# Full-width token norms and a block in front of each down projection, in a streaming-encoder layer on one Trainium2 core

## Chip, cores, metric

One NeuronCore of a Trainium2 chip runs the whole layer. The metric is the device time of one execution in microseconds (us); the table below gives the median of three runs. Engines: PE (TensorE, its weight loads shown as PEld), DVE (VectorE), ACT (ScalarE), POOL (GpSimd), SP (here it only issues DMAs).

## The reference

One layer over 2048 tokens, model width 1024, all in float32:

```python
u = rms_norm(h, g_pre_mix)
z_glu, q, k, v, z_gate = split(u @ w_in)
c = a * sigmoid(b)                              # a, b = halves of z_glu
c = silu(layer_norm(causal_depthwise_conv31(c)))
y_conv = c @ w_conv_out
y_attn = banded_attention(rope(q), rope(k), v, sinks) @ w_attn_out
y = gates[0] * y_conv + gates[1] * y_attn       # gates = sigmoid(z_gate)
h = h + rms_norm(y @ w_out, g_post_mix)
gate, val = split(rms_norm(h, g_pre_ffn) @ w_up)     # 2816 columns each
f = (gelu(causal_depthwise_conv3(gate)) * val) @ w_down
h = h + rms_norm(f, g_post_ffn)
h = h + (p @ w_ple) * sigmoid(h @ w_ple_gate)
```

`rms_norm` divides each token's 1024 values by the root of their mean square (plus 1e-6); `layer_norm` also takes the mean off and runs over the 512 convolution channels.

## The kernel before

The sequence is cut into 4 chunks of 512 tokens (`T`). Activations lie with features on the 128 partitions and the 512 tokens along the free axis, so a width of 1024 is 8 tiles of 128x512. Each float32 product is made of three passes: operand and weight are split into a high part (`_hi`, fp32r) and the rest (`_lo`), and `product` (lines 776 to 780) issues hi x hi, hi x lo and lo x hi. A weight **block** is eight 128x128 tiles, so 24 matmuls of 512 columns; a chunk needs `NB` = 122 blocks. `by_tile` (lines 791 to 812) is the form in which four outputs grow together, one input tile after the other.

**Weight stream.** `block_order` (lines 65 to 80) writes out the order of the 488 blocks by hand, `PLACE` is a block's position, and there are `SLOTS` = 3 buffers. SP loads block n once block n-3 is done (`load_block`, lines 376 to 388). In chunk 0 every block is fresh: one load into `w_stage`, POOL makes `w_hi` (line 429, one cast) and `w_lo` (line 432, four subtractions), and SP stores both for the later chunks, which load the two halves directly. PE counts finished blocks in `block_done`, and ACT and DVE wait for that count (`done(c, b)`).

**Token norms.** A sum over features is a sum over partitions. ACT squares each tile (`square`), DVE adds the squares into `ssum` (`add_square`, line 1232). `token_sums` (line 813) makes, with four one-column float32 matmuls (each issued as two), the sums of the 512 tokens as a 128x4 tile in bank `SMALL`; ACT takes the root (line 446), DVE does six small steps on 128x4 (`norm`, line 1202: reciprocal and one Newton step) and spreads the result into four diagonal matrices `diag` (line 1218). Then `spread` (line 821) multiplies `ones` by `diag`, so that bank `BC` holds each token's factor in all partitions. There are four norms of this kind in a chunk (`LN` of the convolution, `POST` after the mixer, `PRE` before and `PF` after the channel mixer), 16 in all. The norm of the input rows (`x_norm`) works on rows and has no matmul.

**Channel mixer.** 22 up tiles (`up(c, t)`), each two blocks, gate and value. For each one ACT starts the 3-tap convolution (line 609), DVE ends it (lines 1517 to 1522), ACT takes the GELU (612), DVE multiplies by the value (`f_tmp`, 1531), ACT makes `f_hi` (614), DVE `f_lo` (1534); `f_hi` and `f_lo` have 8 slots. The tiles come in three groups, 8, 8 and 6, and behind each stands a down projection, `down(c, q)` (line 972), with 8 output tiles of 8 (last: 6) products, in banks 4 and 5 in turn:

```python
for k in range(count):
    pe.wait_ge(f_lo_ready, c * NF + FB[q] + k + 1)
    at, last = part(0, k)
    ...
    at, last = part(1, k)
```

So its first two output tiles take their products in turn, and need two weight blocks at a time. ACT copies the tiles of the first projection to `acc` (`first_down`, line 617), DVE adds the others (`add_down`, line 1538, the sum at 1544), each after `done(c, dn_done(q, j))`: the weight block that holds the tile's last product is done. DVE's 31-tap convolution of the next chunk (`taps`, line 1288) is put among the up tiles, six taps a tile, and 40 taps and the rotary angles beside the first down projection. Between the second down projection and the third group, PE turns the 512x256 embedding rows `p` (`turn_p`, line 1034, the matmuls at 829) into banks 4 and 5, behind a wait for the last sum.

**End of a chunk.** Behind the third down projection come (chunks 0 to 2) the six query, key and value blocks of the next chunk, with the token sums and the spread of `PF` after the first and the second, then eight projection tiles `p @ w_ple` (`ple_tiles`, line 1040, six matmuls each, two banks in turn), then the gate blocks `B_PG`. ACT copies each projection tile (`ple_evict`, line 625, the copy at 632) into `acc`; DVE adds the normed tiles to `h` (`h3_tile`: lines 1470 and 1475), and ACT and DVE split the new `h` (623, 1554) and do the rotary steps (487, 1328 to 1336) in one hand-written order. All eight copies stand behind the last h tile there. In chunk 3 there is no next chunk; the projection tiles follow the down projection directly.

Of the kernel before, what the change touches and what calls it, by code (L numbers as in the profile page):

```python
# [64 lines left out]
def block_order():  # L65

    order = [(0, b) for b in range(B_GLU, B_GA)]
    for c in range(CHUNKS):
# [61 lines left out]
NORM_AT = {key: n for n, key in enumerate(norm_order())}  # L130
# [16 lines left out]
def build_kernel(nc, x, p, positions, weights, columns, identity, split_weights, out):  # L147
    with ExitStack() as ctx:
# [26 lines left out]
        rows_h = sb("rows_h", [P, TT, D], F32, at + 16 * K)  # L175

# [61 lines left out]
        diag = sb("diag", [P, TT, P], F32)  # L238
# [19 lines left out]
        SMALL, BC = 6, 7  # L258
# [4 lines left out]
        QK_BANK = 0, 2, 1, 3, 4  # L263
# [39 lines left out]

        def xu_bank(c, f):
            return 0 if c else (0, 2, 4, 5)[f % 4]
# [4 lines left out]
        def ple_bank(c, j):  # L310
            return (0, 6 if c + 1 < CHUNKS else 2)[j % 2]

        def ple_tile(c, j):
            return acc[:, j] if c + 1 < CHUNKS else ple_last[:, j]
# [20 lines left out]
        root_ready, norm_step, diag_ready, bc_ready = map(sem, ("root_ready", "norm_step", "diag_ready", "bc_ready"))  # L335
# [18 lines left out]
        dn_first, dn_acc, p_turned, p_hi, p_lo = map(sem, ("dn_first", "dn_acc", "p_turned", "p_hi", "p_lo"))  # L354
# [83 lines left out]
        def _(act):  # L438
# [6 lines left out]
            def root(src, count):  # L445
                copy(n_root[:, :], src, ACT.Sqrt, bias=column("eps"), scale=1.0 / count).then_inc(root_ready, 1)

# [6 lines left out]
            def sum_root(kind, c, count):  # L454
                act.wait_ge(ssum_done, SUM_AT[kind, c] + 1)
                root(ps[:, SMALL, 0:TT], count)

            def x_norm(c):
# [4 lines left out]
                root(x_ss[:, :], D)  # L463
# [18 lines left out]
            def rope_swap(c, j):  # L482
# [3 lines left out]
                for q in range(4):  # L486
                    last = copy(rope_b[32 * q:32 * q + 32, j % 2], ps[32 * (q ^ 1):32 * (q ^ 1) + 32, QK_BANK[j]],
# [115 lines left out]
            def up(c, t):  # L603
# [9 lines left out]
                act.wait_ge(ft_ready, item)  # L613
# [11 lines left out]
            def ple_evict(c, j):  # L625
# [4 lines left out]
                if c + 1 < CHUNKS:  # L630
                    act.wait_ge(h3_step, c * KD_ + j + 1)
# [23 lines left out]
            for c in range(CHUNKS):  # L655
# [49 lines left out]
                for t in range(FB[0], FB[1]):  # L705
                    up(c, t)
                first_down(c)
                if more:
                    sines(c + 1)
                for t in range(FB[1], FB[2]):  # L710
                    up(c, t)
                if more:
                    centred_squares(c + 1, 0, NC)
                for k in range(NP):
                    act.wait_ge(p_turned, c * NP + k + 1)
                    copy(f_hi[:, FN - NP + k], ps[:, PT_BANK + k], ACT.Copy).then_inc(p_hi, 1)
                for t in range(FB[2], FB[3]):
# [1121 lines left out]
```

## Time and profile before

| | us |
|---|---|
| median of 3 runs | 2912.37 (2909.88 to 2916.42) |
| the profiled execution | 2908.04 |
| its span, first to last instruction | 2906.2 |
| PE busy | 2836.1 (98%) |
| PE weight loads busy | 2342.0 (81%) |
| DVE busy | 1391.3 (48%) |
| ACT busy | 807.7 (28%) |
| POOL busy | 512.0 (18%), all in chunk 0 |
| mean granted TensorE clock | 0.994 of full |

Busy time is the time in which at least one instruction of the engine runs. "Idle before" is the time that the engine stood in front of an instruction, with what released it. Starts are counted from the span's start; the first chunk ends at about 840, chunks 1 and 2 take 707 each, the rest is chunk 3.

### The profile page before, as it was taken

What the parts mean: (1) busy time and instruction counts of PE and PEld (TensorE: products, weight loads), DVE (VectorE), ACT (ScalarE), POOL (GpSimd) and SP (SyncE); (2) the same over time, 40 slices, a digit from 0 to 9 for tenths busy, and PEclk for the clock granted to TensorE, in tenths of its full rate; (3) what the DMA queues carried; (4) which work ended last, traced back from release to release, by engine and by line L of the source; (5) the groups of instructions that cost most, each with busy time, mean ns of one, the idle gap of its engine ahead of it and who ended that gap; (6) DMA issues with size and microseconds to landing.
All of it is one profiled execution on the core that took longest, in us unless ns stands there. A gap on an engine that the chain in (4) does not pass through costs nothing.

```text
span 2906.2 us, 32957 instructions
## 1 busy us (share of the span) xinstructions
PE 2836.1 (98%) x12952; PEld 2342.0 (81%) x12952; DVE 1391.3 (48%) x2427; ACT 807.7 (28%) x1541; POOL 512.0 (18%) x614
## 2 busy tenths in 40 slices
PE   7999999999999999999999999999999999999998
PEld 6887887877788888888888888888888887888886
DVE  7786576633642246662344234765335422613235
ACT  3533321111353232111146232211124612211012
POOL 5667277766430000000000000000000000000000
PEclk9999999999999999999999999999999999999999
DMA  6678587767665645554554654555555454555554
GB/s 249 228 252 307 201 288 273 292 253 258 217 240 181 248 164 199 195 196 178 185 187 174 217 205 178 207 188 192 184 188 188 160 196 181 185 198 190 188 188 145
DMA packets 182746, 606.36 MB, mean 209 GB/s; under 512 B 18752, under 2 KB 37440, under 8 KB 182592
## 3 DMA queue, kind: packets, MB, share of 16 engines
q1 hardware_dynamic: 165696, 595.86, 56.4%
q10 hardware_dynamic: 16896, 8.39, 1.0%
q8 instruction: 103, 1.69, 0.2%
q14 instruction: 51, 0.42, 0.0%
HBM read 467.87 MB, written 136.31 MB: 208 GB/s over the span
## 4 chain that ended last, share of the span: by engine, by line
PE 90%; DVE 4%; DMA 2%; POOL 2%; ACT 1%; issue 1%; SPq 0%; DVEq 0%; ACTq 0%
PE ps L778 24%; PE ps L780 24%; PE ps L779 24%; PE ps L802 5%; PE ps L803 5%; PE ps L806 5%; DMA w_stage<-in_weights 2%; POOL w_lo L432 1%; PE ps L829 1%; PE ps L916 1%; DVE h_tmp L1470 1%; DVE h L1475 1%; DVE y_lo L1554 1%; PE ps L873 1%; PE ps L875 1%
## 5 line engine op out<-in xcount | busy, mean ns | idle before, releaser
L778 PE MATMUL ps<-y_hi,w_hi 128*128 128x512 f32 x1536 | 603.2, 393 | 1.2 <-POOL w_lo L432 1.2
L780 PE MATMUL ps<-y_hi,w_lo 128*128 128x512 f32 x1536 | 598.3, 390 | 0.0
L779 PE MATMUL ps<-y_lo,w_hi 128*128 128x512 f32 x1536 | 597.8, 389 | 0.0
L432 POOL TENSOR_TENSOR w_lo<-w_stage,w_hi 128x256 fp32r<-128x256 f32 x488 | 379.4, 809 | 9.8
L778 PEld LDWEIGHTS ps<-y_hi,w_hi 128*128 128x128 f32 x1536 | 288.4, 188 | 61.8 <-DVE f_tmp L1531 1.9
L780 PEld LDWEIGHTS ps<-y_hi,w_lo 128*128 128x128 f32 x1536 | 288.3, 188 | 60.7
L779 PEld LDWEIGHTS ps<-y_lo,w_hi 128*128 128x128 f32 x1536 | 288.5, 188 | 59.5 <-issue 1.0
L778 PE MATMUL ps<-f_hi,w_hi 128*128 128x512 f32 x768 | 304.7, 397 | 20.8 <-POOL w_lo L432 10.6
L1288 DVE SCALAR_TENSOR_TENSOR ps<-conv_in,col,ps 128x512 f32<-128x512 f32 x452 | 310.2, 749 | 0.1
L780 PE MATMUL ps<-f_hi,w_lo 128*128 128x512 f32 x768 | 300.5, 391 | 0.0
L779 PE MATMUL ps<-f_lo,w_hi 128*128 128x512 f32 x768 | 300.5, 391 | 0.0
L778 PE MATMUL ps<-u_hi,w_hi 128*128 128x512 f32 x704 | 278.4, 395 | 0.0
L780 PE MATMUL ps<-u_hi,w_lo 128*128 128x512 f32 x704 | 274.7, 390 | 0.0
L779 PE MATMUL ps<-u_lo,w_hi 128*128 128x512 f32 x704 | 274.5, 390 | 0.0
L778 PEld LDWEIGHTS ps<-f_hi,w_hi 128*128 128x128 f32 x768 | 145.1, 189 | 61.3 <-DVE acc L1544 12.1
L429 POOL CAST w_hi<-w_stage 128x1024 fp32r<-128x1024 f32 x122 | 133.0, 1090 | 311.8 <-DMA w_stage<-in_weights 311.8
L1517 DVE SCALAR_TENSOR_TENSOR g_conv<-ps,col,g_conv 128x511 f32<-128x511 f32 x88 | 65.8, 747 | 230.2 <-ACT g_conv L609 230.2
L780 PEld LDWEIGHTS ps<-f_hi,w_lo 128*128 128x128 f32 x768 | 145.0, 189 | 30.8
L779 PEld LDWEIGHTS ps<-f_lo,w_hi 128*128 128x128 f32 x768 | 145.1, 189 | 30.4 <-issue 1.0
L609 ACT ACTIVATE g_conv<-ps,col 128x512 f32<-128x512 f32 x88 | 68.5, 779 | 338.8 <-PE ps L780 206.3
L802 PE MATMUL ps<-y_hi,w_hi 128*128 128x512 f32 x384 | 152.4, 397 | 10.0 <-ACT ple_last L632 4.1
L1544 DVE TENSOR_TENSOR acc<-acc,ps 128x512 f32<-128x512 f32 x64 | 43.9, 687 | 234.3 <-PE ps L780 234.3
(190 smaller groups left out, 3919.3 us busy)
## 6 DMA issues: line engine op xcount, KB each, us to landing
w_hi<-split_weights SPq DMA_DIRECT2D x366, 512.0 KB, 3.2
w_lo<-split_weights SPq DMA_DIRECT2D x366, 512.0 KB, 4.1
w_stage<-in_weights SPq DMA_DIRECT2D x122, 512.0 KB, 3.7
split_weights<-w_hi SPq DMA_DIRECT2D x122, 512.0 KB, 2.8
split_weights<-w_lo SPq DMA_DIRECT2D x122, 512.0 KB, 4.0
rows_u<-in_x SPq DMA_DIRECT2D x16, 512.0 KB, 5.6
rows_h<-in_x SPq DMA_DIRECT2D x16, 512.0 KB, 5.8
out_h<-o_rows ACTq DMA_DIRECT2D x24, 256.0 KB, 2.8
```

What stands on the lines that cost most here:

```text
L429: nc.gpsimd.tensor_copy(w_hi[:, slot], w_stage[:, slot]).then_inc(w_hi_ready, 1)
L432: last = nc.gpsimd.tensor_tensor(w_lo[:, slot, k:k + 2], w_stage[:, slot, k:k + 2], w_hi[:, slot, k:k + 2].bitcast(F32), ALU.subtract)
L609: copy(g_conv[:, t % 2], ps[:, up_bank(t)[0]], ACT.Identity, bias=column("ffn_b", t), scale=column("ffn_w", 3 * t + 2)).then_inc(tap0_read ...
L778: nc.tensor.matmul(bank, w_hi[:, slot, kk], hi, start=start, stop=False)
L779: nc.tensor.matmul(bank, w_hi[:, slot, kk], lo, start=False, stop=False)
L780: return nc.tensor.matmul(bank, w_lo[:, slot, kk], hi, start=False, stop=stop)
L802: nc.tensor.matmul(ps[:, banks[o]], w_hi[:, slot, first + o], hi[:, k], start=(k == 0), stop=False)
L803: nc.tensor.matmul(ps[:, banks[o]], w_lo[:, slot, first + o], hi[:, k], start=False, stop=False)
L806: last = nc.tensor.matmul(ps[:, banks[o]], w_hi[:, slot, first + o], lo[:, k], start=False, stop=(k == 7))
L1288: V.scalar_tensor_tensor(dst, src, column("conv_w", t + j * TAPS), old, ALU.mult, ALU.add).then_inc(conv_tap, 1)
L1517: V.scalar_tensor_tensor(g_conv[:, n, 1:T], gate[:, 0:T - 1], column("ffn_w", 3 * t + 1), g_conv[:, n, 1:T], ALU.mult, ALU.add).then_inc(t ...
L1544: V.tensor_tensor(acc[:, j], acc[:, j], ps[:, dn_bank(q, j)], ALU.add).then_inc(dn_acc, 1)
```

## The change

- **Norms.** `token_sums` becomes one matmul of `ones` by `ssum`, 512 columns wide, into `BC`: each partition holds all tokens' sums. `spread`, `diag` and the bank `SMALL` go. ACT takes the reciprocal root of `BC` at full width into `r_row` and its square into `sq`; DVE does three full-width steps (scale and shift, multiply, Newton step) and writes the factor back into `BC`. The row norm of `x` stays as it was.
- **Down projections.** PE does the first up tile of the next group (two blocks) before down projections 0 and 1, and the first query block of the next chunk before down projection 2 (chunks 0 to 2); `block_order` follows. A down projection now waits once for all `f_lo` of its group, and makes its tiles one after the other; only the third of the last chunk keeps the paired form. ACT's copy to `f_hi` and DVE's `f_lo` are cut off from the up tile (`up_round`, `up_rest`); for tiles 8 and 16 they follow the down projection that still reads the slots (DVE's angles and taps stand between).
- **Signals.** In the third down projection each tile whose end is not a block's end counts `dn_tile`, and `add_down` waits for that.
- **`turn_p`** moves behind the second up tile of the third group, with its copies.
- **Projection tiles** go to banks 1 and 6 and to memory of their own (`ple_first`, `ple_rest`), so their copies no longer wait for the h steps; ACT makes four of them among the last h tiles. The query blocks use other banks.

The diff, cut to its core:

```diff
@@ block_order
-        order += [(c, b) for b in range(B_UP[0], B_WP)]
+        for q in range(3):
+            ahead = 2 if q < 2 else 0
+            order += [(c, b) for b in range(B_UP[q] + (2 if q else 0), B_DN[q])]
+            order += [(c, B_DN[q] + FN + b) for b in range(ahead)]
+            if c + 1 < CHUNKS and q == 2:
+                order.append((c + 1, B_QKV))
+            order += [(c, b) for b in range(B_DN[q], B_UP[q + 1] if q < 2 else B_WP)]
         if c + 1 < CHUNKS:
-            order += [(c + 1, b) for b in range(B_QKV, B_GA)]
+            order += [(c + 1, b) for b in range(B_QKV + 1, B_GA)]
@@ buffers and banks
+        ple_first = sb("ple_first", [P, 6, T], F32, at + 16 * K)
+        ple_rest = sb("ple_rest", [P, 2, T], F32, at + 8 * K)
-        diag = sb("diag", [P, TT, P], F32)
+        r_row = sb("r_row", [P, T], F32)
+        def qk_bank(c, j):
+            return (1, 3, 0, 2, 4)[j] if c else (0, 2, 1, 3, 4)[j]
         def ple_bank(c, j):
-            return (0, 6 if c + 1 < CHUNKS else 2)[j % 2]
+            return ((1, 6) if c + 1 < CHUNKS else (0, 2))[j % 2]
@@ ACT
             def sum_root(kind, c, count):
                 act.wait_ge(ssum_done, SUM_AT[kind, c] + 1)
-                root(ps[:, SMALL, 0:TT], count)
+                copy(r_row[:, :], ps[:, BC], ACT.Abs_reciprocal_sqrt, bias=column("eps"),
+                     scale=1.0 / count).then_inc(row_root, 1)
+                act.wait_ge(row_root, SUM_AT[kind, c] + 1)
+                copy(sq[:, 0], r_row[:, :], ACT.Square).then_inc(row_square, 1)
+            def up_round(c, t):
+                act.wait_ge(ft_ready, c * NF + t + 1)
+                if t in FB[1:3]:
+                    done(c, dn_done(FB.index(t) - 1, KD_ - 1))
                 copy(f_hi[:, t % 8], f_tmp[:, t % 2], ACT.Copy).then_inc(f_hi_ready, 1)
@@ ple_evict
-                if c + 1 < CHUNKS:
-                    act.wait_ge(h3_step, c * KD_ + j + 1)
@@ ACT, channel mixer
                 for t in range(FB[0], FB[1]):
                     up(c, t)
+                    up_round(c, t)
+                up(c, FB[1])
                 first_down(c)
+                up_round(c, FB[1])
                 if more:
                     sines(c + 1)
...
@@ ACT, end of a chunk
-                    for j in range(1, PAIRS):
+                    for j in range(1, PAIRS - 1):
                         h3_tile(c, 2 * j - 1)
                         h3_tile(c, 2 * j)
                         rope_swap(c + 1, j + 1)
+                    rope_swap(c + 1, PAIRS)
+                    h3_tile(c, 5)
+                    ple_evict(c, 0)
+                    ple_evict(c, 1)
+                    h3_tile(c, 6)
+                    ple_evict(c, 2)
+                    ple_evict(c, 3)
                     h3_tile(c, 7)
                     value_out(c + 1)
-                    for j in range(KD_):
+                    for j in range(4, KD_):
                         ple_evict(c, j)
@@ PE, token_sums; spread is removed
-                for t in range(TT):
-                    last = nc.tensor.matmul(ps[:, SMALL, t:t + 1], ssum[:, P * t:P * t + P], ones[:, 0:1],
-                                            start=True, stop=True)
-                last.then_inc(ssum_done, 1)
+                nc.tensor.matmul(ps[:, BC], ones[:, :], ssum[:, :], start=True, stop=True).then_inc(ssum_done, 1)
@@ PE, down
+                paired = q == 2 and c + 1 == CHUNKS
+                if paired:
...
+                else:
+                    pe.wait_ge(f_lo_ready, c * NF + FB[q + 1])
+                for j in range(2 if paired else 0, KD_):
...
                         if at % 8 == 7:
                             last.then_inc(block_done, 1)
+                        elif k == count - 1:
+                            last.then_inc(dn_tile, 1)
@@ PE, channel mixer and after
-                for t in range(2, FB[1]):
+                for t in range(2, FB[1] + 1):
                     up(c, t)
                 down(c, 0)
-                for t in range(FB[1], FB[2]):
+                for t in range(FB[1] + 1, FB[2] + 1):
                     up(c, t)
                 down(c, 1, between=(lambda: conv_mean(c + 1)) if more else None)
-                turn_p(c)
-                for t in range(FB[2], FB[3]):
+                for t in range(FB[2] + 1, FB[3]):
+                    if t == FB[2] + 2:
+                        turn_p(c)
...
+                if more:
+                    pe.wait_ge(ft_ready, (c + 1) * NF - 1)
+                    full_block(c + 1, B_QKV, qk_bank(c + 1, 0), u_hi, u_lo)
                 down(c, 2)
...
@@ DVE
+            def token_norm(kind, c, count):
+                at = SUM_AT[kind, c]
+                dve.wait_ge(ssum_done, at + 1)
+                dve.wait_ge(row_root, at + 1)
+                V.tensor_scalar(ssum[:, :], ps[:, BC], -0.5 / count, -0.5 * EPS, ALU.mult, ALU.add).then_inc(row_step, 1)
+                dve.wait_ge(row_step, 2 * at + 1)
+                dve.wait_ge(row_square, at + 1)
+                V.tensor_tensor(ssum[:, :], ssum[:, :], sq[:, 0], ALU.mult).then_inc(row_step, 1)
+                dve.wait_ge(row_step, 2 * at + 2)
+                V.scalar_tensor_tensor(ps[:, BC], ssum[:, :], 1.5, r_row[:, :], ALU.add, ALU.mult).then_inc(bc_ready, 1)
+                dve.wait_ge(bc_ready, at + 1)
@@ DVE, add_down
-                done(c, dn_done(q, j))
+                if q == 2 and j % 4 != 3 and not (j == 0 and c + 1 == CHUNKS):
+                    tiles = [t for t in range(KD_) if t % 4 != 3]
+                    dve.wait_ge(dn_tile, c * len(tiles) + tiles.index(j) + (1 if c + 1 < CHUNKS else 0))
+                else:
+                    done(c, dn_done(q, j))
@@ DVE, channel mixer
+                    up_rest(c, t, among)
+                up(c, FB[1])
                 if more:
                     angles(c + 1)
                     taps(40)
...
+                up_rest(c, FB[1])
```

## Rows read from the trace of the kernel before

**Rows 1.** The page, part 1: busy us (share of the span) xinstructions.

```profile
PE 2836.1 (98%) x12952; PEld 2342.0 (81%) x12952; DVE 1391.3 (48%) x2427; ACT 807.7 (28%) x1541; POOL 512.0 (18%) x614
```

**Rows 2.** PE's waits over the whole span: us in total, times, longest us.

```profile
PE ps L778 <- POOL w_lo L432: 12.4, 7, 2.9
PE ps L778 <- ACT acc L632: 5.3, 3, 4.5
```

**Rows 3.** Timeline of PE, chunk 1: start us, us, line, op, xcount, idle before.

```profile
1462.11 0.39 PE L780 MATMUL ps<-u_hi,w_lo 128*128 128x512 f32 x1
1462.34 0.94 PE L817 MATMUL ps<-ones,ssum 128*128 128x1 f32 x8
...
1463.47 0.40 PE L779 MATMUL ps<-u_lo,w_hi 128*128 128x512 f32 x1
...
1468.73 1.02 PE L824 MATMUL ps<-diag,ones 128*128 128x512 f32 x2
...
1469.83 0.40 PE L779 MATMUL ps<-u_lo,w_hi 128*128 128x512 f32 x1
```

**Rows 4.** Groups by form; timeline of ACT; a stretch of chunk 1 (PE, PEld, DVE).

```profile
L467 ACT ACTIVATE u_hi<-ps,col 128x512 fp32r<-128x512 f32 x32 | 22.1, 695 | 48.0 <-PE ps L829 48.0
...
L1470 DVE SCALAR_TENSOR_TENSOR h_tmp<-acc,col,ps 128x512 f32<-128x512 f32 x64 | 47.1, 742 | 24.4 <-PE ps L824 24.4
...
2837.45 1.28 ACT L446 ACT_TABLE_LOAD   x1
2838.74 0.27 ACT L446 ACTIVATE n_root<-ps,col 128x4 f32<-128x4 f32 x1
...
1215.30:1221.30 6.00, 6.00 (x29) 4.95 (x28) 0.00 (x0) 0.60 (x1) 0.00 (x0) 1.00 0.46 175
```

**Rows 5.** The chain that ended last, in chunk 0: start us, us, what.

```profile
384.96 7.61 DMA w_stage<-in_weights
...
582.02 3.19 DMA w_stage<-in_weights
...
585.27 1.05 POOL w_hi L429
...
586.39 2.80 POOL w_lo L432 x4
```

**Rows 6.** PE's waits near 440, 580, 700 us; a stretch: us, busy, PEclk, DMA, GB/s.

```profile
PE ps L778 <- POOL w_lo L432: 4.6, 2, 2.9
...
PE ps L778 <- POOL w_lo L432: 3.8, 2, 2.0
...
PE ps L778 <- POOL w_lo L432: 2.2, 1, 2.2
...
700.00:735.00 35.00, 31.73 (x130) 25.11 (x129) 10.66 (x15) 5.21 (x8) 22.80 (x28) 0.95 0.67 239
```

**Rows 7.** PE's waits, 1300 to 1362 and 1415 to 1460 us; timeline of PE.

```profile
PE ps L778 <- DVE acc L1544: 0.2, 1, 0.2
...
PE ps L778 <- DVE acc L1544: 1.0, 2, 0.8
...
1354.55 0.52 PE L829 MATMUL ps<-ident,p_rows 128*128 128x128 f32 x3 [0.94 <-DVE acc L1544]
```

**Rows 8.** Projection tiles and last norm: PE, clock, h sums (min/median/max ns), DVE.

```profile
785.91 0.79 PE L778 MATMUL ps<-f_hi,w_hi 128*128 128x512 f32 x1 [4.46 <-ACT acc L632]
...
785.00:795.00 10.00, 9.09 (x31) 7.32 (x32) 5.71 (x6) 3.74 (x7) 4.48 (x4) 0.73 0.34 108
...
L1475 DVE TENSOR_TENSOR h<-h,h_tmp x64: 678/690/1517, 329.8 to 2860.8; 128x512 f32<-128x512 f32 x64
...
2837.29 1.05 PE L817 MATMUL ps<-ones,ssum 128*128 128x1 f32 x8 [0.78 <-DVE ssum L1232]
...
2844.81 0.75 DVE L1470 SCALAR_TENSOR_TENSOR h_tmp<-acc,col,ps 128x512 f32<-128x512 f32 x1 [4.00 <-PE ps L824]
...
2851.64 0.53 PE L802 MATMUL ps<-y_hi,w_hi 128*128 128x512 f32 x1 [4.11 <-ACT ple_last L632]
```

More of the change, by code:

```diff
@@ L462, in x_norm @@
                     act.wait_ge(x_squared, c * TT + t + 1)
-                root(x_ss[:, :], D)
+                copy(n_root[:, :], x_ss[:, :], ACT.Sqrt, bias=column("eps"), scale=1.0 / D).then_inc(root_ready, 1)
             def u_tile(c, f):
@@ L1059, in _ @@
                         gate_b_block(c, 2 * i, between=(lambda: token_sums(LN, 0)) if i == 3 else None)
-                        gate_b_block(c, 2 * i + 1, between=(lambda: spread(LN, 0)) if i == 3 else None)
+                        gate_b_block(c, 2 * i + 1)
                         if i == 2:
@@ L1107, in _ @@
                     pe.wait_ge(y2_out, c * KD_ + KD_)
-                    glu_pair(c + 1, 3, between=lambda: spread(PRE, c))
+                    glu_pair(c + 1, 3)
                 else:
                     token_sums(POST, c)
-                    spread(POST, c)
                 pe.wait_ge(y2_out, c * KD_ + KD_)
@@ L1532, in up, with up_rest @@
                 taps(among[1])
-                dve.wait_ge(f_hi_ready, item)
-                V.tensor_tensor(f_lo[:, t % 8], f_tmp[:, n], f_hi[:, t % 8].bitcast(F32),
+            def up_rest(c, t, among=0):
+                dve.wait_ge(f_hi_ready, c * NF + t + 1)
+                V.tensor_tensor(f_lo[:, t % 8], f_tmp[:, t % 2], f_hi[:, t % 8].bitcast(F32),
                                 ALU.subtract).then_inc(f_lo_ready, 1)
-                taps(among[2])
+                taps(among)
             def add_down(c, q, j):
@@ L1667, in _ @@
                 for t in range(FB[0], FB[1]):
-                    up(c, t, (2, 2, 2) if more and t + 1 < FB[1] else (0, 0, 0))
+                    among = 2 if more and t + 1 < FB[1] else 0
+                    up(c, t, (among, among))
+                    up_rest(c, t, among)
+                up(c, FB[1])
                 if more:
@@ L1671, in _ @@
                     taps(40)
-                for t in range(FB[1], FB[2]):
-                    up(c, t, (2, 2, 2) if more and t + 1 < FB[2] else (0, 0, 0))
+                up_rest(c, FB[1])
+                for t in range(FB[1] + 1, FB[2]):
+                    among = 2 if more else 0
+                    up(c, t, (among, among))
+                    up_rest(c, t, among)
+                up(c, FB[2])
                 if more:
```

132 lines of the change are left out of this document (59 added, 73 removed).

## The prediction, made before the change was run

> **What bounds the kernel now.** The page comes first: PE is busy for 2836.1 of 2906.2 us [rows 1]. The other engines are under half, so the time is PE's own work plus the 70 us in which it stands. Next come PE's waits over the whole span [rows 2]: the largest after the start is 12.4 us for POOL's `w_lo`, the second half of a weight block that is split on its first use (chunk 0 only); then 5.3 us for copies of the projection tiles. The timeline of PE gives the unit of all that follows: 512-column matmuls start 0.227 us apart (1462.11 to 1462.34) although each lasts 0.39 [rows 3], so 24 of them, one weight block, take 5.44 us, and a stop costs its idle time plus 0.16 (0.39 less 0.227). Anything not on PE counts only where PE waits for it.
>
> **Token norms.** Before, a norm costs PE two visits. The eight one-column matmuls start at 1462.34, and the second matmul after them at 1463.47: 1.13, less 0.227 for the one between, is 0.90. The spread takes from 1468.73 to 1469.83, less 0.227: 0.87 [rows 3]. After, one full-width matmul of the spread's form is left: 0.87. So each norm whose visits stand among other PE work gives back 0.90. There are 16. I count 13: the first LayerNorm is left out, since the blocks behind it wait for weights, and the last post-mix and last post-FFN norms are counted by their chains. 13 x 0.90 = **11.8 us**.
>
> The root and three steps move to full width. ACT: one PSUM activation at 0.70, then a Square beside DVE's first step. DVE: three steps of at most 0.74 [rows 4]. With 1.02 for the matmul this is 3.9 us from the sum to the factor (bounds 3.3 and 6: half a microsecond either way for form, and one extra table load of 1.28). It needs no second place in PE's order, which before came a block (5.4 us) or more later, so in chunks 0 to 2 the factor comes about 2 us earlier than now; no consumer becomes late. DVE's waits for root and square have only the small halo copy, the zeroing and the h tiles queued behind them, which needed the factor anyway. ACT's load of the root table is 1.28 at 2837.45, and the root starts at 2838.74, at once behind it [rows 4]; it is issued ahead of the wait for the sum. I add no term for it. The Trainium skill's page "ScalarE: Activation LUTs" (What ACT_TABLE_LOAD costs) gives 2.66 us for every switch, load and drain; the trace shows no such drain in front of the root, and by the page's figure my sum would be about 1.4 us smaller, at the last norm alone.
>
> **Pairs of down tiles in chunk 0.** The first two tiles of a down projection took products in turn and needed two weight blocks at once. A slot comes free when the block three places earlier is done, so the second of the pair has one block (5.44) instead of two (10.9) for its chain. At the pair before 589.43 that chain is load 3.19, POOL 1.05 and 2.80, with 0.4 for signals 7.4 [rows 5]; less 5.44 it gives the stop of 2.0 seen there. The same comes back two blocks later. The waits are 4.6, 3.8 and 2.2 us [rows 6], five stops, 11.4 with 0.16 each. After the third the clock falls: 0.95 of full over 35 us [rows 6], 1.75 us lost. Sum **13.1 us**. Tile after tile, a block has 10.9 for a chain of 7.4 to 8.3, so the stops go (the 8.3 from the longest of them, 2.9). The first two blocks of the next up quarter (each one load, one split, two stores on SP) move ahead of the down blocks; count and pace stay. A slow load is the 7.61 seen once [rows 5]: a chain of 11.8, a stop of about 1. I take none and keep three for the range.
>
> What the pairing covered was the last `f_lo`. Now PE waits for all of a group's `f_lo`, but has done an up tile (10.9 us) or a query block (5.44) since, against about 2.5 us from the end of a value block to `f_lo` (three operations of at most 0.75 and signals, an estimate from rows 4). Cost nothing, unless DVE is over 3 us behind. The added waits: ACT takes the copy of tile 8 after the eight evictions and of tile 16 after down projection 1, because the slots of `f_hi` are still read. Behind them stand the sines and the next up tile, which ACT needs 5.44 us later; its work there is under 4 us. DVE's angles and 40 taps fill most of a down projection, but in its last 6.0 us DVE is idle beside a busy PE [rows 4]; they start as early as before.
>
> **Waits within and behind down tiles.** In every chunk the third projection has two stops with 1.0 us of idle time, the larger before tile 4, since tile 2's sum is taken only when a whole weight block is done [rows 7]: 1.0 + 2 x 0.16 = 1.3. The second projection stops for 0.2 (0.36 with its 0.16), in chunk 3 alike. Turning `p` waits 0.94 + 0.16 = 1.10 for the last sum, four times [rows 7]. Own signals, single tiles and the move behind an up tile remove these, except 0.3 in the last chunk, whose third projection stays paired: 4 x (1.3 + 0.36 + 1.1) - 0.3 = **10.7 us**. A first stop in down 0 is at most 0.17; left out.
>
> **Projection tiles.** In chunk 0 PE stands 4.46 us for the first copy, behind the last h tile on ACT, and resumes at the low clock: 0.73 on the mean of 10 us [rows 8], that is 5.4 us at 1.2 GHz, 4.5 of them busy, which lose 2.2. With 0.16 this is 6.8 us. In chunks 1 and 2 it is 0.4 + 0.16 each. After, seen from the token sum, PE comes here 5.44 + 0.87 = 6.3 us sooner, as one query block went ahead of the down projection, and the h chain about 2 sooner. So the copies are 4.3 later in relation, but four of them now precede the last h tile, worth four tiles of 1.36 = 5.4. Chunks 1 and 2: 0.4 + 4.3 - 5.4 is negative, the wait goes: **1.1 us**. Chunk 0: 4.46 + 4.3 - 5.4 = 3.3, and more, because the h steps fall deeper into POOL's splits: an h sum takes 0.69 in the median and up to 1.52 [rows 8], and I add 1.7 for two more groups of such steps. So 5.0 is left and **1.8 us** gained (between -2 and +6.8).
>
> **Last norm.** The tile sum before it comes sooner by its own signal, so the 0.78 idle before the token sums goes (with 0.16). ACT's load ends at 2838.74 as now, the chain of root and three steps takes 2.9, so the h tiles start at 2841.6 instead of 2844.81, and the stop of 4.11 at 2851.64 shrinks with them [rows 4, 8]: **3.2 us**. The last post-mix norm has zeroing and edge steps that now follow the chain instead of lying beside the spread: nothing, within 0.9 either way.
>
> **Sum.** 11.8 + 13.1 + 10.7 + 1.1 + 1.8 + 3.2 = 41.7. The profiled execution took 2908.0 us (span 2906.2 and 1.8 around it), which gives 2866.3. It is 4.4 below the median of the runs, 2912.4, so the median should be **2870.7 us**.
>
> **The rivals.**
> (a) Chunk 0 keeps most of its weight stops. For it: the splits run at every block and one load took 7.61. Against it: in the down projections of chunk 0 only pair starts wait for POOL [rows 6]. The 13.1 shrinks to 3: 2881.
> (b) Chunk 0 stays clean at the projection too, because four early copies suffice: 5 us more, and the low clock at the end may go (1.5): 2864. For it: the wait sits three tiles before the end of the stage. The Trainium skill's page "SBUF — State Buffer" (Who interferes with whom) speaks against it: a DVE instruction with two SBUF inputs waits for the whole of a POOL instruction that reads SBUF. By that rule, the wait stays; the 1.52 against 0.69 [rows 8] agrees.
> (c) Slower: the norm chain becomes PE's wait. The place is the pre-FFN and post-FFN norm of chunks 0 to 2, where u2 or h tiles feed the next streaming product. Cover there is two blocks (10.9) after the sum, less 1.4 for the first tile's two steps; so it decides from a chain of 9.5. To cancel 41.7 over six norms and lose 6 more each must stand 8 us: a chain of 17.5 instead of 3.9. Only full-width steps at over four times the rows' durations would do it: 2919.
> (d) The change does less than it says: the stops are hidden work, a wait behind each (DVE's order of add, square, copy) takes its place, and only the norms' PE time is gained: 2901.
>
> **How the numbers follow.** Forecast 0.73, (a) 0.11, (b) 0.10, (c) 0.03, (d) 0.03. A measurement of this kernel can tell 0.2%, 5.8 us, from no change. All but (c) lie beyond it on the fast side; some mixture of (a) and (d) with new stops could end within it: faster 0.95, same 0.02, slower 0.03. The range takes (b) and (a) in, with 3 us for the spread of runs: 2861 to 2883.
>
> **What would show it.** Right: PE's waits for POOL fall from 12.4 to about 2 (the stop behind the slow load of rows 5 stays); no stop at a down start; 16 double matmuls with `ones` and `ssum` for norms, none with `diag`; PE busy lower by about 14 us of norm work; turning `p` without idle; a stop of 3 to 5 us before the seventh projection tile of chunk 0. Wrong: PE waiting for `f_lo`, for `h_tmp` steps, or for `w_lo` inside down projections; activation table loads rising well above those of before and standing behind the sum; a granted clock below 0.99.

## The result and the profile after

The kernel after takes 2861.66 us in the median (2860.9 to 2865.01); the ratio to before is 0.9826 [0.9811, 0.9842], 51 us less. Its profiled execution has a span of 2859.2 us (2861.0 with what lies around it), 47.0 below the span of before; 41.7 were forecast. The rest of the difference of the medians is the choice of executions: the profiled one of before lay 4.3 below the median of 2912.37, that of after 0.7 below its own.

The page after, busy time and instructions; then that of PE's waits over the whole span (us in total, times, longest us):

```profile
PE 2809.0 (98%) x12824; PEld 2326.5 (81%) x12824; DVE 1401.9 (49%) x2363; ACT 828.3 (29%) x1560; POOL 515.7 (18%) x614
```

```profile
PE ps L848 <- DVE rows_u L1262: 19.3, 1, 19.3
PE ps L830 <- ACT y_hi L612: 8.2, 4, 7.0
PE ps L806 <- ACT ple_first L645: 3.8, 2, 2.3
PE ps L830 <- ACT ple_last L645: 3.1, 1, 3.1
...
PE ps L806 <- POOL w_lo L443: 1.6, 3, 0.6
...
PE ps L830 <- POOL w_lo L443: 0.7, 2, 0.5
...
PE ps L806 <- DVE acc L1575: 0.2, 1, 0.2
```

The same view of the kernel before had these rows beside the two of [rows 2]:

```profile
PE ps L778 <- DVE acc L1544: 4.9, 12, 0.8
...
PE ps L829 <- DVE acc L1544: 3.8, 4, 0.9
...
PE ps L802 <- POOL w_lo L432: 1.2, 2, 0.8
```

For POOL PE stood 13.6 us before (12.4 of [rows 2] and 1.2) and stands 2.3 now (1.6 and 0.7), none of it in a down projection. The 4.9 and 3.8 us that PE stood for sums (`acc`) are one wait of 0.2, in the last chunk's paired projection. In place of 5.3 us for projection tiles [rows 2] there are 3.8, two waits in chunk 0; one of 0.3 is new in the last chunk. The 7.0 for `y_hi` is not new: at the last chunk's post-mix norm PE stood 2.15 before the spread and 3.01 before the tiles, and now has one stop.

A token norm, on PE's timeline of chunk 1 (start, us, line, op, count), answers to [rows 3]:

```profile
1437.56 0.39 PE L808 MATMUL ps<-u_hi,w_lo 128*128 128x512 f32 x1
1437.79 1.02 PE L844 MATMUL ps<-ssum,ones 128*128 128x512 f32 x2
1438.24 0.80 PE L806 MATMUL ps<-u_hi,w_hi 128*128 128x512 f32 x1
1438.88 0.40 PE L807 MATMUL ps<-u_lo,w_hi 128*128 128x512 f32 x1
```

From 1437.79 to the second matmul after it, 1438.88, is 1.09; less 0.227 for the one between, 0.86: one visit at the forecast price.

To see where the time went I cut each span at the first score product of every chunk (the matmuls that read `k_dup`). All later readings use this table, in us; chunk 3 ends with the span, and the part ahead of chunk 0's cut (105 to 107) is left out.

| kernel | chunk 0 | chunk 1 | chunk 2 | chunk 3 | span |
|---|---|---|---|---|---|
| before | 735.1 | 706.8 | 706.8 | 652.4 | 2906.2 |
| after | 710.2 | 698.7 | 698.7 | 645.2 | 2859.2 |
| e1_two_visit_norms | 719.2 | 703.4 | 703.4 | 647.8 | 2879.8 |
| e2_pairs | 726.9 | 699.9 | 699.9 | 644.2 | 2877.6 |
| e3_copies_last | 718.2 | 706.3 | 706.4 | 643.4 | 2880.4 |
| e4_none_ahead | 719.1 | 709.2 | 707.7 | 655.6 | 2897.6 |
| e5_block_signals | 715.5 | 699.8 | 699.8 | 645.2 | 2865.8 |
| e6_turn_early | 711.8 | 699.8 | 699.8 | 647.5 | 2864.7 |
| b2_mid | 704.6 | 698.6 | 698.6 | 645.2 | 2853.6 |
| b1_best | 704.7 | 698.6 | 698.6 | 637.8 | 2846.9 |

Chunk 0 gave 24.9, but the kernel after comes 1.3 later to the cut ahead of it, and before loses as much behind that cut, 1.0 of it to five matmuls at the low clock: at the first token sum both kernels are even (222.67 and 222.63). So chunk 0 with the start gave 23.6, chunks 1 and 2 8.1 each, chunk 3 7.2. The forecast by the same cuts was 21.3 (norms 3.6, pairs 13.1, waits 2.8, projection 1.8), 6.9, 6.9 and 6.5.

### The profile page after: what moved, and what is told of

Its sections match the earlier page's. It is cut to its first block, busy times and chain, and to the rows that moved or that the text cites. A ratio compares the mean times of both kernels' runs of the same rounds, so it can differ in the third digit from the quotient of the medians.

```text
span 2859.2 us, 32678 instructions
## 1 busy us (share of the span) xinstructions
PE 2809.0 (98%) x12824; PEld 2326.5 (81%) x12824; DVE 1401.9 (49%) x2363; ACT 828.3 (29%) x1560; POOL 515.7 (18%) x614
## 4 chain that ended last, share of the span: by engine, by line
PE 93%; DVE 3%; DMA 1%; ACT 1%; POOL 1%; issue 1%; SPq 0%; DVEq 0%; ACTq 0%
PE ps L806 25%; PE ps L808 25%; PE ps L807 25%; PE ps L830 5%; PE ps L834 4%; PE ps L831 4%; DMA w_stage<-in_weights 1%; PE ps L848 1%; PE ps L935 1%; POOL w_lo L443 1%; PE ps L892 1%; PE ps L894 1%; PE ps L924 0%; PE ps L844 0%; PE ps L907 0%
```

## The experiments

Theory A was the prediction's: each part of the change takes away stops that can be named, at idle time plus 0.16. Its rivals differ by run and stand in the expectations. The spans are of one profiled execution of each kernel; that of e1 was its slowest of four, 2.7 us above its own median.

Chunk 0 needs care. Up to the token sum at 320 us the edits of e2 to e6, b2 and b1 change nothing, yet from the chunk's cut to that sum these executions differ: against the kernel after by -0.7 us in e2, +1.1 in e3, +4.5 in e4, +4.0 in e5, +0.9 in e6, -0.1 in b2 and +0.6 in b1. In e4 and e5 PE stops there for POOL for 1.8 us, at 282 and 281 us, with 7 matmuls at the low clock behind it. From that sum to the end of the chunk, which is what an edit did, the differences are 17.3 in e2, 6.9 in e3, 4.4 in e4, 1.2 in e5, 0.6 in e6, -5.5 in b2 and -6.1 in b1.

### e1: norms with two visits again

```diff
@@ PE: token_sums, and spread(kind, c) put back one block or more behind it (ACT's root, DVE's small steps and diag too)
-                nc.tensor.matmul(ps[:, BC], ones[:, :], ssum[:, :], start=True, stop=True).then_inc(ssum_done, 1)
+                for t in range(TT):
+                    last = nc.tensor.matmul(ps[:, SMALL, t:t + 1], ssum[:, P * t:P * t + P], ones[:, 0:1],
+                                            start=True, stop=True)
+                last.then_inc(ssum_done, 1)
...
+            def spread(kind, c):
+                pe.wait_ge(diag_ready, SUM_AT[kind, c] + 1)
+                nc.tensor.matmul(ps[:, BC], ones[:, :], diag[:, :, :].rearrange("p t n -> p (t n)"),
+                                 start=True, stop=True).then_inc(bc_ready, 1)
```

> The changed kernel with the token norms of before: one-column sums, small steps, diag and spread, at their old places in PE's order. Theory A (PE's own time was saved): 13 norms among other PE work cost 0.90 us more each (11.8), the last norm 2.3 to 3.2 more; span 2859.2 + 14 to 15 = 2873 to 2874, and each of the chunks 1 and 2 longer by 3.6 (from 698.7 to 702.3). Rival B (the factor's earlier arrival also took waits away): then PE waits for DVE's h or u2 steps appear in chunks 1 and 2 and these grow by more than 5. Rival C (the norms bring nothing, the rest of the change does it): under 3 us in all.

Measured: 2878.9 us in the median, ratio 0.989 [0.9875, 0.9904], span 20.6 above after, where theory A had 14 to 15. Chunks 1 and 2 are 4.7 longer. Set against the kernel after matmul by matmul, the starts of chunk 1 are 3.8 later ahead of the projection, 0.94 for each of the four norms, and 1.0 more is lost at two stops that were not in my sum. PE's timeline of this run, near the projection of chunk 1:

```profile
1476.02 0.50 PE L803 MATMUL ps<-f_hi,w_hi 128*128 128x512 f32 x1 [0.46 <-ACT ple_first L642]
...
1481.68 0.50 PE L803 MATMUL ps<-f_hi,w_hi 128*128 128x512 f32 x1
```

The factor now comes later than with full-width steps, the h tiles with it, and the copies behind them miss PE by 0.46 (0.62 with its 0.16); the second matmul shown starts 0.07 late as well, and behind each of the two the next one follows 0.34 later instead of 0.227. In chunk 0 it is the same at a larger scale: PE stands 3.05 and 2.45 us there instead of 1.47 and 2.29. So the narrow PE work is worth what was forecast and a little more, and the full-width chain also buys the projection 1.7 us of idle time in chunk 0 and 1.0 us in each middle chunk: some of rival B beside theory A. The forecast had the earlier factor as a gain in relation, but had put no price on losing it.

### e2: every down projection paired again

```diff
@@ PE, down
-                paired = q == 2 and c + 1 == CHUNKS
+                paired = True
```

> The changed kernel with the first two tiles of every down projection made in turn again, all else kept. Theory A (the pair needs a weight block one place too early): in chunk 0 the stops for w_lo come back at the starts and two blocks later, 1.8 to 2.9 us each, 11 to 13 us together with their restarts, and in chunks 1 and 2 only the stop of 0.4 in tile 2 (three times each, 1 us a chunk). Span 2871 to 2875. Rival B (the block ahead, not the single tiles, removed the weight stops, because it keeps POOL ahead): chunk 0 grows by under 3 us, span 2863 to 2866. Rival C (f_lo was the reason for the stops): chunks 1 and 2 would grow like chunk 0.

Measured: 2880.44 us, ratio 0.9899 [0.9883, 0.9916], span +18.4, above the 12 to 16 of theory A. Of that 16.7 lies in chunk 0 and 1.3 in each of chunks 1 and 2, where nothing is split. PE's waits over the whole span:

```profile
PE ps L806 <- POOL w_lo L443: 10.9, 6, 2.5
```

and three stretches of chunk 0 (us, busy of PE, PEld, DVE, ACT, POOL, PEclk, DMA share, GB/s), of this run, and the last of them of the kernel after:

```profile
440.00:500.00 60.00, 56.02 (x231) 45.13 (x230) 44.45 (x68) 7.05 (x11) 39.82 (x50) 0.94 0.68 255
599.00:619.00 20.00, 18.08 (x77) 14.41 (x78) 3.07 (x5) 0.00 (x0) 9.05 (x12) 1.00 0.46 172
700.00:735.00 35.00, 32.69 (x136) 26.27 (x135) 7.91 (x11) 3.88 (x7) 21.75 (x26) 0.95 0.59 213
```

```profile
700.00:735.00 35.00, 35.00 (x154) 28.65 (x153) 11.51 (x16) 6.99 (x10) 15.82 (x20) 1.00 0.75 272
```

The pairs alone bring the weight stops back, and single tiles had taken all of them: rival (a) is out. Less the 1.3 that chunks 1 and 2 show they cost 15.4 here (16.0 counted from the token sum at 320 us), where 13.1 were forecast. The five stops at pair starts hold 10.2 us of idle time (10.6 in before [rows 6]), but after three of them the granted clock falls, 1.4 to 1.6 us each; in before it fell after one.

### e3: all eight copies behind the last h tile again

```diff
@@ ACT, end of a chunk
                     h3_tile(c, 5)
-                    ple_evict(c, 0)
-                    ple_evict(c, 1)
                     h3_tile(c, 6)
-                    ple_evict(c, 2)
-                    ple_evict(c, 3)
                     h3_tile(c, 7)
                     value_out(c + 1)
-                    for j in range(4, KD_):
+                    for j in range(KD_):
```

> The changed kernel with all eight copies of the projection tiles behind the last h tile on ACT, as before. Theory A (with a query block moved ahead, the projection tiles come about 4.3 us earlier against the h chain): PE stops before the third tile for 0.4 + 4.3 = 4.7 us in chunks 1 and 2, and for 8 to 10 in chunk 0, where 4.1 of stops and 1.4 of low clock stand now; span + 4.7 x 2 + 4 = 2872 to 2876, and more if the low clock follows a stop of that length (1.5 to 2 each). Rival B (the copies' place is without effect since the last h tile's copy comes early enough): under 3 us in all.

Measured: 2881.07 us, ratio 0.9896 [0.9881, 0.991], span +21.2 (13 to 17 expected, more with the low clock): 8.0 in chunk 0, 7.6 and 7.8 in chunks 1 and 2. PE's timeline of chunk 1, and two stretches behind it:

```profile
1475.97 0.79 PE L802 MATMUL ps<-f_hi,w_hi 128*128 128x512 f32 x1 [5.01 <-ACT ple_first L645]
```

```profile
1476.00:1481.00 5.00, 5.00 (x12) 3.93 (x13) 2.81 (x5) 1.00 (x2) 0.00 (x0) 0.51 0.00 0
1481.00:1486.00 5.00, 5.00 (x24) 4.13 (x23) 0.00 (x0) 2.39 (x4) 0.00 (x0) 1.00 0.58 210
```

The kernel before stood 0.4 us at this place with the same order of copies. What differs is the query block, which the change took from behind the third down projection to before it: PE is here one block earlier. So in chunks 1 and 2 the early copies mostly pay for the cover that the new order takes. This is argued from three kernels (before: 0.4; e3: 5.0; e4, where the query block lies behind the projection and the copies are early: none); none has the old place of both in an otherwise new kernel. The forecast's relation was 4.3 us later and 5.4 regained: 0.4 + 4.3 = 4.7 without the copies, and 5.0 stands here. To the 5.0 come 0.16 and 2.2 to 2.4 of low clock, 12 matmuls in the stretch of 5 us at 0.51 where the next has 24.

### e4: no block in front of a down projection

```diff
@@ PE, channel mixer (ACT, DVE and block_order follow)
-                for t in range(2, FB[1] + 1):
+                for t in range(2, FB[1]):
                     up(c, t)
                 down(c, 0)
...
-                if more:
-                    pe.wait_ge(ft_ready, (c + 1) * NF - 1)
-                    full_block(c + 1, B_QKV, qk_bank(c + 1, 0), u_hi, u_lo)
                 down(c, 2)
```

> The changed kernel without a block ahead of the down projections, the down tiles still one after the other. Theory A (the block ahead covers f_lo of the last up tile): eleven projections stop for about 2.2 us idle plus 0.26 restart each, 27 us, minus nothing; each of the chunks 1 and 2 longer by 7 to 8; span 2884 to 2888. In chunk 0 the weight stops of before do not come back. Rival B (DVE and ACT finish f_lo while PE is still in its queue, the block ahead buys nothing, only the single tiles do): within 3 us of 2859. Rival C (the block ahead is what the weight stream needs): chunk 0 grows by 10 more than the others.

Measured: 2897.97 us, ratio 0.9953 [0.9939, 0.9968], span +38.4, some 10 to 14 more than expected. PE's waits, whole span; then its timeline at two of the stops and three stretches:

```profile
PE ps L796 <- DVE f_lo L1549: 26.1, 11, 2.9
```

```profile
1297.52 0.50 PE L796 MATMUL ps<-f_hi,w_hi 128*128 128x512 f32 x1 [2.17 <-DVE f_lo L1549]
...
1872.12 0.50 PE L796 MATMUL ps<-f_hi,w_hi 128*128 128x512 f32 x1 [2.17 <-DVE f_lo L1549]
```

```profile
1297.50:1302.50 5.00, 4.98 (x22) 4.13 (x23) 1.96 (x3) 0.00 (x0) 0.00 (x0) 1.00 0.36 143
1872.10:1877.10 5.00, 4.98 (x15) 3.98 (x16) 4.72 (x10) 0.00 (x0) 0.00 (x0) 0.66 0.35 138
2546.40:2553.40 7.00, 6.94 (x18) 5.50 (x19) 0.01 (x1) 0.00 (x0) 0.00 (x0) 0.56 0.17 65
```

All eleven down projections that are made tile by tile wait 2.2 to 2.9 us for the last `f_lo`, near the 2.5 that the prediction estimated from the end of a value block. This is what the block in front hides, and the price of single tiles without it. The stops with 0.16 each are 27.9, less 3.5 that PE no longer stands at chunk 0's projection (its second stop is gone, the first is 0.4: the query block lies behind the down projection again). The excess is the clock: stops of one length, 2.17, are followed by full clock at 1297.5 and by 0.66 at 1872.1, and one of 2.9 in the last chunk by 0.56. Behind stops there are 82 matmuls 0.427 apart instead of 0.227, in the kernel after 21: 61 times 0.2 is 12.2 us. Seven of the 82 follow the stop for POOL at 282 us, which this edit doesn't touch.

### e5: sums taken at the block's signal

```diff
@@ DVE, add_down
-                if q == 2 and j % 4 != 3 and not (j == 0 and c + 1 == CHUNKS):
-                    tiles = [t for t in range(KD_) if t % 4 != 3]
-                    dve.wait_ge(dn_tile, ...)
-                else:
-                    done(c, dn_done(q, j))
+                done(c, dn_done(q, j))
```

> Edit: the kernel after, with the third down tiles' sums taken at the signal of the whole weight block instead of their own; nothing else differs. Theory A (own signals are what removed the stops): a third tile has six products, so tile 2 ends six products before its block does, and tile 4, which uses the same bank, starts right there; PE stands about 1.0 us before tile 4 as in the kernel before, with 0.16 and a restart of 0.1 that is 1.25 us in each of the four chunks. In the last chunk the sums of tiles 6 and 7 then fall together at the end of the projection, 0.7 us more before the token sum. Span 5 to 6.5 us above the 2859.2 of the kernel after: 2864 to 2866. Theory B (tile after tile alone removed the stops, the signals do nothing): within 1 us of 2859.2. Theory C (a longer stop brings the low clock with it): more than 8 us above.

Measured: 2866.39 us, ratio 0.9839 [0.9826, 0.9853], span +6.6. PE's timeline, chunk 1:

```profile
1421.35 0.50 PE L806 MATMUL ps<-f_hi,w_hi 128*128 128x512 f32 x1 [0.85 <-DVE acc L1571]
1421.69 0.40 PE L807 MATMUL ps<-f_lo,w_hi 128*128 128x512 f32 x1
```

The stop before tile 4 is back. Chunks 1 and 2 are 1.1 longer each: 0.85, 0.16, and 0.1 because the next matmul follows after 0.34 and not 0.227. That last is the restart. Of the 5.2 that chunk 0 is longer, 4.0 lie ahead of the token sum at 320 us and are not the edit's; behind it 1.2 are left, the same stop. In chunk 3 both expected stops are there, 0.85, and 0.78 before the token sum, and yet it takes 645.2 as before the edit, chiefly since behind its stop of 3.13 the clock stayed full. So the span met the expectation of 5 to 6.5 above by luck; each chunk by itself bears out theory A.

### e6: `p` turned right behind down projection 1

```diff
@@ PE, channel mixer (ACT's and DVE's copies move along)
-                    if t == FB[2] + 2:
+                    if t == FB[2] + 1:
                         turn_p(c)
```

> Edit: the kernel after, with the p tiles turned directly behind down projection 1 instead of one up tile later, and their copies on ACT and DVE moved along; nothing else differs. Theory A (the turn waits for the last sum of the down projection): 0.94 us idle before the turn, with 0.16 and a restart of 0.1 that is 1.2 us in each of four chunks, 4.8 in all: span 2863.5 to 2865. Theory B (the sum comes in time now that single tiles end evenly, the place doesn't matter): within 1 us of 2859.2. Theory C (the copies now lie ahead of the up tile's evictions and PE waits for these too): 8 us or more.

Measured: 2865.08 us, ratio 0.9839 [0.9825, 0.9852], span +5.5. PE's timeline, chunk 1:

```profile
1340.04 1.06 PE L848 MATMUL ps<-ident,p_rows 128*128 128x128 f32 x8 [0.94 <-DVE acc L1575]
```

Idle 0.94 as in [rows 7], and 1.10 longer in chunks 1 and 2, the prediction's 0.94 + 0.16 to the hundredth; the 1.2 expected here had a restart of 0.1 that doesn't show in front of these short matmuls. Chunk 0 is 0.6 longer behind the token sum. Chunk 3 lost 2.4; its stop is the same 0.94, and what is more is low clock after stops that both kernels have, 25 matmuls at 0.427 against 14.

### b2 and b1: the stops that are left

What PE still stood for after the change, beside the start and the last chunk's norms, was ACT's copies at the two projections. b2 changes chunks 0 to 2; PE's wait for a copy then goes three tiles back instead of two:

```diff
@@ ple_bank
-            return ((1, 6) if c + 1 < CHUNKS else (0, 2))[j % 2]
+            return (1, 6, 3)[j % 3] if c + 1 < CHUNKS else (0, 2)[j % 2]
@@ ACT, end of a chunk
                     h3_tile(c, 6)
-                    ple_evict(c, 2)
-                    ple_evict(c, 3)
+                    for j in range(2, KD_):
+                        ple_evict(c, j)
                     h3_tile(c, 7)
                     value_out(c + 1)
-                    for j in range(4, KD_):
-                        ple_evict(c, j)
```

> The middle-chunk part of the best version alone (three banks for projection tiles, copies 2 to 7 ahead of the last h tile, in chunks 0 to 2). Theory A: both stops of chunk 0 go, chunk 0 is 5.5 us shorter, chunks 1 to 3 stay at 698.7, 698.7 and 645.2: span 2853 to 2854.5. Theory B (the last h tile, now behind six copies, comes late for the product that reads it, or the stop comes back three tiles later): chunk 0 within 2 us of its 710.2 and chunks 1 and 2 no shorter or up to 2 us longer: 2857 to 2863.

Measured: 2855.76 us (2855.44 to 2856.58), ratio 0.9805 [0.9791, 0.9818]. A stretch of chunk 0 with its projection:

```profile
700.00:800.00 100.00, 100.00 (x442) 82.31 (x441) 58.24 (x72) 40.68 (x66) 60.49 (x66) 1.00 0.69 254
```

No idle time in 100 us, chunk 0 is 5.6 shorter (5.5 expected), the others unchanged. The h steps still lie among POOL's splits, so the late steps could be covered. b2 has a third bank and a new order on ACT together; which of the two took how much of the stops wasn't run.

b1 adds the last chunk: its post-mix norm with the edge steps ahead of it and the zeroing behind the first residual; at the end other banks, h tile 0 ahead of copies 4 and 5, and PE's wait for all copies moved behind the first gate tile.

```diff
@@ DVE, last chunk's post-mix norm
+                if not more:
+                    edges(c)
                 token_norm(POST, c, D)
@@ ACT, last projection
-                    for j in range(2, 6):
+                    for j in range(1, 4):
...
-                        if j in (1, 2):
-                            ple_evict(c, j + 5)
+                        for k in ((4, 5), (6,), (7,))[j] if j < 3 else ():
+                            ple_evict(c, k)
@@ PE
-                    pe.wait_ge(ple_out, c * KD_ + KD_)
...
+                pe.wait_ge(ple_out, c * KD_ + KD_)
```

> A version meant to beat both kernels. Three edits to the kernel after. Middle chunks: projection tiles use three banks in place of two, so PE runs three tiles ahead of the copies, and all of copies 2 to 7 stand ahead of the last h tile: this takes the two stops of chunk 0 (1.47 and 2.29 us idle, with 0.16 each, a restart, and the low clock behind the second): about 5.5 us. Last chunk's end: other banks, h tile 0 ahead of copies 4 and 5, PE's wait for all copies moved behind the first gate tile: the 0.3 and 3.1 us stops shrink to about 0.5 in all, and with them the low clock behind the longer: about 4.5 us. Last post-mix norm: edge steps ahead of the norm, zeroing behind the first residual: its chain is shorter by about 0.9, and the three small stops behind it (0.4 each) shrink: 1 to 2.5 us. Theory A (these are the stops that are left, each worth idle + 0.16 and what the clock loses): 11 to 13 us below 2859.2, span 2846.5 to 2849.5, median 2848.5 to 2851.5. Theory B (the stops move on to the next wait of the same chain, ACT being late by its work and not by its order): less than 5 us below, 2854 or more.

Measured: 2849.15 us (2847.95 to 2849.71), ratio 0.9781 [0.9768, 0.9795]: 12.5 below the kernel after. The page, then PE's waits from 750 us on:

```profile
PE 2806.2 (99%) x12824; PEld 2326.9 (82%) x12824; DVE 1397.5 (49%) x2363; ACT 828.9 (29%) x1560; POOL 516.0 (18%) x614
```

```profile
PE ps L827 <- ACT y_hi L612: 6.0, 1, 6.0
PE ps L841 <- DVE ssum L1245: 2.0, 1, 2.0
PE ps L904 <- DVE h L1595: 1.2, 1, 1.2
PE ps L803 <- ACT ple_last L645: 0.5, 1, 0.5
...
```

Both copies' waits of the middle and the 3.1 of the end are 0.5 in all, and the post-mix stop is 6.0 instead of 7.0, without the three small ones behind it. Chunk 3 gave 7.4. The parts of the last chunk were not run one by one.

## Why the prediction was right, and what it mis-sized

The stops that the prediction named as going away went, and e2, e5 and e6 brought theirs back one group at a time; only the stop at the last norm shrank by less than said. The size was less good. The median lies 9.0 us below the forecast of 2870.7 and only 0.7 above the lower end of the range. 5.3 of the 9.0 are terms that were too small, named below; 3.7 are that 4.4 us between profiled execution and median were carried over from before, where after shows 0.7, which is the chance of single executions. By its number the median would sooner speak for rival (b), 2864; the traces don't, since chunk 0 kept stops at its projection.

**Token norms: right.** 0.86 for the visit that stayed, 0.87 forecast, and by e1 0.94 for the one that went, 0.90 forecast; four in a chunk are 3.8 instead of 3.6. Rival (c) didn't come near: no wait for the chain stands in chunks 0 to 2. The first LayerNorm, which I had left out because the blocks behind it wait for weights, gave 0.8 too: the next token sum starts at 320.12 instead of 320.94.

**The last norm: 3.2 forecast, 2.3 found.** ACT and DVE at the last norm of the kernel after:

```profile
2791.80 0.60 ACT L645 ACTIVATE ple_last<-ps 128x512 f32<-128x512 f32 x1 [0.76 <-PE ps L808]
2792.41 1.28 ACT L464 ACT_TABLE_LOAD   x1
2793.71 0.69 ACT L464 ACTIVATE r_row<-ps,col 128x512 f32<-128x512 f32 x1
2794.43 0.63 ACT L467 ACTIVATE sq<-r_row 128x512 f32<-128x512 f32 x1
...
2798.74 0.60 ACT L645 ACTIVATE ple_last<-ps 128x512 f32<-128x512 f32 x1 [0.78 <-PE ps L808]
2799.23 0.62 ACT L638 ACTIVATE y_hi<-h 128x512 fp32r<-128x512 f32 x1
```

```profile
2794.50 0.69 DVE L1229 TENSOR_SCALAR ssum<-ps 128x512 f32<-128x512 f32 x1 [3.21 <-ACT r_row L464]
2795.23 0.69 DVE L1232 TENSOR_TENSOR ssum<-ssum,sq 128x512 f32<-128x512 f32 x1
2795.95 0.70 DVE L1234 SCALAR_TENSOR_TENSOR ps<-ssum,r_row 128x512 f32<-128x512 f32 x1
2796.74 0.75 DVE L1495 SCALAR_TENSOR_TENSOR h_tmp<-acc,col,ps 128x512 f32<-128x512 f32 x1
```

From root to first h tile are 3.0 us (2793.71 to 2796.74), for 2.9 forecast. From the start of the sum's matmul on PE to the h tile it is 5.14 now (2791.60 to 2796.74) where it was 7.52 [rows 8]. But of these 2.4 only 1.4 reached PE: ACT took `y_hi` behind the copy of tile 5, which waits for a product of PE's (2798.74). The sum's stop before it (0.94) went. The step that failed is "the stop of 4.11 shrinks with them": it shrank to 3.13, by 1.0. In b1, with the h tile ahead of copies 4 and 5, other banks and PE's wait for all copies moved, only 0.5 is left; the three were not run apart. The table load starts 0.01 us behind the copy ahead of it, and the root 0.02 behind the load. By the Trainium skill's page "ScalarE: Activation LUTs" (What ACT_TABLE_LOAD costs) a drain would stand with the load, 2.66 together. The trace doesn't agree: there is no room for one on either side of this load, and the load alone is 1.28.

**The last post-mix norm: 0 forecast, 0.6 found**, from sum to next product 8.13 (2415.78 to 2423.91) instead of 8.75; within the 0.9 allowed. Behind it two more small stops stand than before, which cost 1.0; about as much came from 7 matmuls at the low clock where before had 12.

**Chunk 0: 21.3 forecast, 23.6 found.** The weight stops went as forecast, and the low clock behind one of them. The step that failed is "a stop costs its idle time plus 0.16". That is so up to the next matmul, but the one after comes late as well (0.34 for 0.227 in e5), and some ten stops went: 1 us. Beside it stand the first LayerNorm with 0.8 and the stop behind the slow load of [rows 5], which I had left in: 1.17 us before, 0.42 after. The projection gave 0.7 less than its 1.8 (below). That is 1.9 of the 2.3 that are over, and 0.2 are the norms at 0.94.

**Chunks 1 and 2: 6.9 forecast, 8.1 found.** The idle times of before are all gone, as e5 and e6 show each by itself (1.1 and 1.1). What is over can be placed in chunk 1. 0.2 are the norms. 0.6 are restarts: the four stops in front of full-width matmuls cost 0.49, 0.47, 1.16 and 0.73, counted over the next ten starts, where idle time plus 0.16 gives 0.36, 0.33, 1.01 and 0.59. And 0.3 are a stop that the prediction named and left out, the first in down projection 0. It is too short for the view of waits; PE's timeline of the kernel before has it:

```profile
1188.32 0.39 PE L780 MATMUL ps<-f_hi,w_lo 128*128 128x512 f32 x1
1188.72 0.50 PE L778 MATMUL ps<-f_hi,w_hi 128*128 128x512 f32 x1
1189.05 0.40 PE L779 MATMUL ps<-f_lo,w_hi 128*128 128x512 f32 x1
```

From 1188.32 to 1189.05 are 0.73 where two spacings are 0.45. The failed step is the same one as in chunk 0, and the left-out term of "at most 0.17" measured 0.3. About 0.1 stays open.

**Projection tiles: the sum near, its form not.** Chunk 0 was to keep 5.0 with its 0.16, before the seventh tile. PE's timeline:

```profile
760.33 0.50 PE L806 MATMUL ps<-f_hi,w_hi 128*128 128x512 f32 x1 [1.47 <-ACT ple_first L645]
...
768.38 0.79 PE L806 MATMUL ps<-f_hi,w_hi 128*128 128x512 f32 x1 [2.29 <-ACT ple_first L645]
```

It kept two stops, 1.47 and 2.29, that is 4.1 with 0.16 each, and 1.4 of low clock behind the second: 5.5, where before had 6.6 (4.46, 0.16 and ten matmuls at low clock). The stop split in two, and before the seventh tile 2.29 stands where 3 to 5 were named. Rival (b), a clean projection, failed here. The Trainium skill's page "SBUF — State Buffer" (Who interferes with whom), by which a DVE instruction with two SBUF inputs contends with a GpSimd instruction that reads SBUF, was named against it. The rows agree as far as they go: in the kernel after an h sum takes up to 1.19 us in chunk 0, where POOL splits, and 0.70 at most behind it. But in b2 it takes up to 1.43 and PE has no stop, so the rule told of slower steps and not of a wait that must stand.

**PE's busy time: 14 us less named as a sign, 27.1 found.** The norms are 14 to 15 of it. The rest, by the sums above an estimate, is what stops leave in busy time: 0.16 and the restart at each, and matmuls at the low clock.

**The two sides of the change.** e1, e2, e3, e5 and e6 each undo one part, and together they cost 72 us where the whole change brought 47, by the profiled spans; by the medians it is 64 where the change brought 51. Two parts are hardly gains of their own: the early copies (21.2) mostly mend what the query block in front opened, and the block in front (e4, 38.4) mends what single tiles opened. A part's price when taken out of the new kernel is no share of the gain.

## What to carry to other kernels

Where two tiles in turn need two weight blocks at once, make them one after the other and put a block of other work in front, so that the last operand's chain is covered; then count again who now reaches its next wait earlier, and move that wait's work too. Price a stop on a PE-bound kernel at its idle time, 0.16 and 0.1 for the restart, and take up to 2.8 us, the most seen here, for each stop of about 2 us or more as the low clock's risk. Read a difference in a stretch that the edit doesn't touch before reading one where it does: here it reached 4.5 us. Write every part's gain as a stop at a place in a chunk: then single experiments can be read chunk by chunk, far below what the medians resolve.

## What was not expected of the hardware

The granted clock after a stop is not a function of that stop's length. In e4 six stops of 2.17 us, at places of the same kind, had full clock three times and 7 or 8 matmuls 0.427 apart (1.2 GHz) three times. In the kernels with one and the same stop of 6.95 us in the last chunk's post-mix norm, 7 to 12 matmuls followed at that distance; behind the stop of 3.13 at the end none in four kernels, and 7, 8 or 13 in three. That is up to 2.8 us between executions of equal work, more than the smallest parts here are worth. Past the start, no run of three or more such matmuls followed a stop shorter than 1.79 us.
